# A hybrid attention and expert block on one core: x by feature columns instead of token rows, and half of its normalisation moved into the first block of experts

## The reference

```python
xn = rmsnorm(h, ln)              # h = meta tokens and x; y = x * rsqrt(mean(x*x) + 1e-6) * gain
proj = xn @ w_in                 # q, k, v of both attentions (stick-breaking, sliding window)
o = concat(rmsnorm(o_a), rmsnorm(o_b)); h = h + o @ w_out
# then, in blocks of 128 tokens (peer_ffn):
q = tb @ w_query;  top 16 of 128x128 expert pairs for each of 8 heads -> 128 experts a token
act = gelu(u[idx] . tb);  out = sum(softmax * act * v[idx])
h = rmsnorm(h + out, final_norm)
```

## Time and profile before

| | |
|---|---|
| times of three runs | 2914.4, 2919.9, 2925.72 us |
| the profiled execution | 2919.07 us, its span 2917.0 us |
| mean granted clock of TensorE | 0.878 |
| busy share of the span | PE 76%, DVE 75%, POOL 45%, ACT 39% |
| the chain that ended last, by engine | DMA 33%, PE 29%, DVE 23%, ACT 8%, issue 4%, POOL 2% |
| moved | 1155.22 MB, of which the gathers 1073.81 MB |

### The profile page before, as it was taken

How to read it: one execution, slowest core, us unless ns; L and a number is a source line. 1 busy time by engine, 2 the same in 40 slices (tenths; PEclk the granted TensorE clock), 3 DMA queues, 4 the chain that set the end, 5 groups by cost and what they waited for, 6 DMA issues and landing times.

```text
span 2917.0 us, 30220 instructions
## 1 busy us (share of the span) xinstructions
PE 2214.7 (76%) x9182; PEld 950.5 (33%) x9182; DVE 2184.8 (75%) x5506; ACT 1145.3 (39%) x2673; POOL 1316.1 (45%) x1126
## 2 busy tenths in 40 slices
PE   9989888788887988867887777867755775665556
PEld 7564532345333453313322332212311231111111
DVE  4189887786777868679786888779776987668555
ACT  3523377433563335633575326733212331121111
POOL 0024355444554435544565445644444444444442
PEclk9999999899999999979998898988877898767778
DMA  8279999999999999999999999999999999999997
GB/s 320 95 303 409 386 410 418 401 412 380 412 397 419 411 398 414 366 419 419 419 415 417 421 413 409 408 410 418 421 420 422 420 404 421 418 421 411 422 421 321
DMA packets 198096, 1155.22 MB, mean 396 GB/s; under 512 B 23648, under 2 KB 53792, under 8 KB 66480
## 3 DMA queue, kind: packets, MB, share of 16 engines
q0 software_dynamic: 147456, 1073.81, 89.6%
q1 hardware_dynamic: 50480, 79.50, 7.5%
HBM read 1138.21 MB, written 15.01 MB: 395 GB/s over the span
## 4 chain that ended last, share of the span: by engine, by line
DMA 33%; PE 29%; DVE 23%; ACT 8%; issue 4%; POOL 2%; SPq 0%; ACTq 0%; DVEq 0%; POOLq 0%
DMA r_uv<-in_experts,r_wk 31%; PE ps L1868 13%; DVE r_uv L1430 11%; PE ps L1540 4%; PE ps L1786 2%; ACT r_uv L1016 2%; PE ps L1764 2%; PE ps L1534 2%; ACT L1013 2%; POOL r_uv L756 1%; DVE r_wk L1201 1%; DVE r_wk L1199 1%; DVE r_wk L1202 1%; PE ps L1556 1%; DMA r_wk<-lq_dram 1%
## 5 line engine op out<-in xcount | busy, mean ns | idle before, releaser
L756 POOL DMA_INDIRECT r_uv<-in_experts,r_wk x1024 | 1212.8, 1184 | 1406.1 <-PE ps L1868 1191.8
L1868 PE MATMUL ps<-r_uv 128*64 128x512 f32 x4096 | 1234.5, 735 | 668.6 <-ACT r_uv L1016 655.8
L1430 DVE CUSTOM_DVE_ANT_0 r_uv<-r_uv,hnrep 128x1024 f32<-128x1024 f32 x1024 | 1253.8, 1240 | 548.4 <-DMA r_uv<-in_experts,r_wk 539.4
L1868 PEld LDWEIGHTS ps<-r_uv 128*64 128x64 f32 x4096 | 291.1, 157 | 1409.7 <-ACT r_uv L1016 943.9
L1013 ACT ACTIVATE r_wk<-r_wk 128x2 f32<-128x2 f32 x512 | 103.9, 203 | 1446.5 <-DVE r_wk L1430 1445.0
L1016 ACT ACTIVATE r_uv<-gid,r_wk 128x64 f32<-128x64 f32 x684 | 200.7, 340 | 11.6 <-ACT r_wk L1013 0.3
L1013 ACT ACT_TABLE_LOAD x138 | 177.1, 1283 | 2.5
L777 ACT ACT_TABLE_LOAD x117 | 150.1, 1283 | 8.1 <-PE ps L1744 3.7
L1540 PE MATMUL ps<-r_uv,stream_chunk 128*128 128x256 f32 x560 | 134.1, 394 | 3.8 <-DMA stream_chunk<-in_w_chunks 3.8
L1786 PEld LDWEIGHTS ps<-r_wk,r_wq 128*128 128x128 f32 x1024 | 119.6, 193 | 37.0 <-issue 36.5
L1786 PE MATMUL ps<-r_wk,r_wq 128*128 128x128 f32 x1024 | 128.7, 280 | 0.3 <-ACT r_wk L933 0.3
(11 more groups left out here) (181 smaller groups left out, 2217.1 us busy)
## 6 DMA issues: line engine op xcount, KB each, us to landing
r_uv<-in_experts,r_wk POOLq DMA_INDIRECT x1024, 13.5
stream_chunk<-in_w_chunks SPq DMA_DIRECT2D x30, 512.0 KB, 8.0
r_wk<-lkv_dram SPq DMA_DIRECT2D x72, 128.0 KB, 7.5
r_uv<-in_x SPq DMA_DIRECT2D x8, 512.0 KB, 10.3
r_wo<-in_w_chunks SPq DMA_DIRECT2D x8, 512.0 KB, 11.1
r_wk<-in_x SPq DMA_DIRECT2D x8, 512.0 KB, 8.2
r_wo<-in_w_out SPq DMA_DIRECT2D x8, 512.0 KB, 9.5
r_wq<-in_w_query SPq DMA_DIRECT2D x8, 512.0 KB, 6.8
```

What stands on the lines that cost most here:

```text
L756: g.indirect_dma_start(uv[:, SLOT[G], :], None, experts, bass.IndirectOffsetOnAxis(idx[b % 2][:, k:k + 1], 0)).then_inc(rows_in[SLOT[G]], 16)
L1430: v.tensor_tensor_reduce(uv[:, slot, 0:D], uv[:, slot, 0:D], hnrep[:, k % GRP, :], 1.0, 0.0, ALU.mult, ALU.add, actv[:, k:k + 1]).then_inc ...
L1868: last = t_.matmul(ps[HALF * j:HALF * j + HALF, i, :], uv[:, slot, 0:HALF], uv[:, slot, D + 512 * i:D + 512 * i + 512], start=n == 0, stop ...
```

## The change

x is given twice: as before, for the residual, and by columns, features on the partitions (`first_columns` for the tokens 0 to 255 and the meta tokens, `columns` for the other 768). A transposition on PE is not needed any more. ACT squares the columns; PE sums the squares over the partitions with a matrix of ones, which leaves each token's sum on all partitions; ACT and DVE take the root of 128x272 or 128x256 equal rows; DVE scales the columns in place by gain and root. For tokens 256 to 511 DVE first adds the eight features of a partition, and PE sums once. The tokens 512 to 1023 are not touched in the first stage. Their columns (2 MB) are loaded into slots 2 and 3 in block 0, ahead of the keys of unit 13 (units count from 0); they are squared at groups 54 to 56, summed at 55 to 57, their root is taken at 58 and they are scaled at 60 and 61. `NARROW` falls from 56 to 46. The store to `xs_dram` and its load are gone.

```diff
-ONE_MORE, NARROW, WIDE = 43, 56, STREAM_BLOCKS * NG
+FAR_LOAD, FAR_ROOT, FAR_SCALE = 13, 58, (60, 61)
+FAR_SQUARES = {54: (0, 1, 2), 55: (3, 4), 56: (5, 6, 7)}
+FAR_SUMS = {n + 1: cs for n, cs in FAR_SQUARES.items()}
+ONE_MORE, NARROW, WIDE = 43, 46, STREAM_BLOCKS * NG
...
# SP
-            load_x(0)
+            for h in range(DC // 2):
+                e.dma_start(xn0[:, 2 * h:2 * h + 2, :], first_columns[:, 2 * h:2 * h + 2, :]).then_inc(x_in[h], 16)
+            load_chunk(0)
             e.dma_start(cst[:, :], consts).then_inc(consts_in, 16)
...
-                    e.dma_start(xs_dram, r_uv[:, 4 * D:8 * D]).then_inc(xs_out, 16)
...
+                    if (b, u) == (0, FAR_LOAD):
+                        gate(e, "sp", rows_used, NB + max(G for G in range(K) if SLOT[G] in (2, 3)) + 1)
+                        e.dma_start(xnT[:, 1:3, :, :], columns[:, 1:3, :, :]).then_inc(xs_in, 16)
...
# ACT
+            def square_first(h):
+                act.wait_ge(x_in[h], 16)
+                a.activation(sq_columns[0][:, 2 * h:2 * h + 2, :], xn0[:, 2 * h:2 * h + 2, :], ACT.Square).then_inc(squared, 1)
+            def root_columns(tb):
...
+                a.activation(r, sums, ACT.Ln, scale=1.0 / n, bias=epscol).then_inc(logged, 1)
+                act.wait_ge(logged, tb + 1)
+                a.activation(r, r, ACT.Exp, scale=-0.5).then_inc(rooted, 1)
...
+                if s == 2:
+                    square_next()
+                if s == 4:
+                    root_columns(1)
...
# DVE
+            polish_columns(0, ps[:, 2, 0:GW + META], D)
+            dve.wait_ge(consts_in, 16)
+            scale_columns(xn0, r_columns[0])
+            dve.wait_ge(squared, DC // 2 + 2)
+            v.tensor_reduce(sq_next_sum, sq_columns[1].rearrange("p c n -> p n c"), AX.X, ALU.add).then_inc(next_reduced, 1)
+            polish_columns(1, ps[:, 3, 0:GW], D)
+            scale_columns(xnT[:, 0, :, :], r_columns[1])
...
+                    if b == 0 and n in FAR_SCALE:
+                        h = FAR_SCALE.index(n)
+                        if h == 0:
+                            polish_columns(2, ps[:, 7, :], -D)
+                        scale_columns(xnT[:, 1 + h, :, :], r_columns[2][:, GW * h:GW * h + GW])
...
# PE
+            def sum_far(c):
...
+                gate(pe, "pe", far_squared, c + 1)
+                t_.matmul(ps[:, 7, :], negones, sq_far[c], start=c == 0, stop=c == DC - 1).then_inc(far_summed, 1)
...
-            idle_products(11)
-            for k in range(2):
-                turn_rows(k)
-            idle_products(6)
+            pe.wait_ge(ones_set, 1)
+            idle_products(12)
+            sum_first()
+            idle_products(12)
```

More of the change, by code:

```diff
@@ L240, in settle, with block_program @@
             self.n = 0
-def block_program(nc, x, meta, w_chunks, w_v, consts, rope_cs, w_out, sinks, w_query, keys_t, experts, out):
+def block_program(nc, x, first_columns, columns, w_chunks, w_v, consts, rope_cs, w_out, sinks, w_query, keys_t, experts, out):
     with ExitStack() as ctx:
@@ L417, in block_program @@
         gain_spread = sem("gain_spread")
[L418 to L420 removed]
+        ones_set, xs_in = sem("ones_set"), sem("xs_in")
+        x_in = [sem(f"x_in{i}") for i in range(DC // 2 + 1)]
+        squared, col_summed, xT_ready = sem("squared"), sem("col_summed"), sem("xT_ready")
+        logged, rooted, next_reduced = sem("logged"), sem("rooted"), sem("next_reduced")
+        far_squared, far_summed = sem("far_squared"), sem("far_summed")
         v_summed, v_kept, zeroed = sem("v_summed"), sem("v_kept"), sem("zeroed")
@@ L813, in keep_values @@
                     a.activation(own_values, ps[0:rows, 6, 0:P], ACT.Copy).then_inc(v_kept, 1)
-            for k in range(5):
-                square_rows(k)
+            for h in range(DC // 2):
+                square_first(h)
+            root_columns(0)
             def keep_piece(i):
@@ new lines, in scale_columns @@
+            def scale_columns(columns, r):
+                for c in range(DC):
+                    last = v.scalar_tensor_tensor(out=columns[:, c, :], in0=columns[:, c, :], scalar=lnmix[:, c:c + 1], in1=r,
+                                                  op0=ALU.mult, op1=ALU.mult)
+                    if columns is xn0:
+                        last.then_inc(xT_ready, 1)
+                if columns is not xn0:
+                    last.then_inc(xT_ready, 1)
+            polish_columns(0, ps[:, 2, 0:GW + META], D)
@@ L1955 @@
     given = [
-        ("x", np.asarray(x)[0]), ("meta", np.asarray(meta_tokens)), ("w_chunks", w_chunks),
+        ("x", x), ("first_columns", rows(np.concatenate([x[0:GW], np.asarray(meta_tokens)]).T)),
+        ("columns", rows(x[GW:].T).reshape(P, DC, -1, GW).transpose(0, 2, 1, 3)), ("w_chunks", w_chunks),
         ("w_v", rows(np.concatenate([m[:, w * i:w * i + w] for i in range(PAIRS) for m, w in ((va, P), (vb, FAR))], axis=1))), ("consts", consts),
```

160 lines of the change are left out of this document (77 added, 83 removed).

## The result

The changed kernel takes 2933.8 us (median of 14 runs, 2926.2 to 2949.9) against 2919.8 for the kernel before in the same session (2913.7 to 2930.3). The ratio is 1.0047, 95% interval 1.0031 to 1.0063: 13.7 us slower (0.0047 x 2919.9). 2917 was predicted, with a range from 2906 to 2930: the kernel became slower where a small gain was forecast.

The account below looks back on a forecast made before the run. Once gathers run, memory sets the pace; before, PE's list does. From the profiled 2919.07, minus 4.6 (start) plus 2.0 (late block 0) gives 2916.5; that execution was 0.8 under the median, so 2917, range 2906 to 2930.

Parts of the forecast that it names:

- The first stage, -4.6: Start of the kernel to the turned keys: earlier first piece and no transpositions, less the second sum's wait, 4.6 us earlier.
- The rival that the start gives more: First stage saves 8.9 us and the starved stretch of block 0 regains 3.0, giving 2908; chance 0.20.
- The second sum, +2.1: Behind the third piece in the first stage: PE waits 1.6 us for DVE's reduction and needs 0.46 for its product.
- the reason given with the bound: DVE's second-sum reduction reads with a step of 256 words, at a rate not shown; twice as slow adds 2.3 us.
- The ring, +1.7: Late in block 0: seven slots instead of nine for ten groups, some 50 us, cost 1.7 us.
- Unit 13, up to 8: Block 0: unit 13's keys land behind the 2 MB load, so PE may stand for up to 8 us.
- the cover: Late in block 0: about 7.8 us of transfers queued ahead of a gather, hiding shorter stalls if the queue has refilled.
- The late part as a whole, +2.0: Late block 0: fewer slots, keys behind the load and bursts on ACT, PE and DVE together lose 2.0 us.
- far bound of 20: Late block 0 if nothing is hidden: 8 us at unit 13 and 4 + 4 + 4 of bursts, 20 us lost.
- the late bursts outrun the queue: Rival: at unit 13 and from group 54 on, delays exceed the queue's cover, giving 2925 to 2935; chance 0.22.
- Blocks 1 to 7: Nothing is changed there; any loss in these blocks would show the forecast wrong.

Follow-up runs that it names:

- e3: Kernel before with seven slots instead of nine from group 46, nothing else changed: ratio 1.0015.
- e4: Kernel before with seven slots from group 46 and its 2 MB load moved ahead of unit 13's keys: ratio 1.0018.
- e5: Changed kernel with load and squares of tokens 512 to 1023, but without their sums, root and scaling: ratio 1.0007.
- e6: Changed kernel without DVE's polishing and scaling of tokens 512 to 1023; squares, sums and root stay: ratio 1.0033.
- e13: Changed kernel with nine slots to the end of block 0, no 2 MB load, and the late work done on query-weight columns: ratio 0.9995.
- e1: Changed first stage with the late part of the kernel before (nine slots until group 56, load behind last keys); tokens 512 to 1023 unnormalised: ratio 0.9994.
- e10: e8 with the keys table loaded ahead of chunk 8 and DVE polishing at step 12 from ACT's copy of the sum: ratio 0.9986.
- e14: Changed kernel's first stage and seven slots from group 46, without 2 MB load and without late work: ratio 0.9995.
- e12: Changed kernel's first stage with nine slots to the end of block 0, without 2 MB load and without late work: ratio 0.9985.
- e7: Changed kernel, complete, with the 2 MB load issued on ACT's queue at group 46 instead of SP's queue: ratio 1.0046.
- e2: Changed kernel without squares, sums, root and scaling of tokens 512 to 1023; seven-slot ring and early load stay: ratio 1.0021.
- e16: Changed kernel with its late work spread: one square at each of groups 49 to 56, root at 58, scaling over 59 to 62: ratio 1.004.
- e8: Kernel before with all x normalised by columns in the first stage, then stored and reloaded as before; second sum one piece later: ratio 1.0002.
- e9: e1 with PE's second sum of squares one piece later, behind the fourth piece: ratio 0.9991.

## Why the prediction was wrong, by its steps

The measured time lies 16.8 us over the forecast (2933.8 against 2917). By the ratios 13.5 of them belong to the late part (15.5 where 2.0 were forecast) and 2.8 to the start (1.8 kept to the end where 4.6 were forecast); the second of these is inside its interval.

**The first stage, -4.6: right where the clock holds, too large on the mean.** The sum was made for the turned keys. In twelve traces with this first stage they start at 42.4 us on the mean, in the three with the old one (before, e3, e4) at 45.2: 2.8 earlier. In four of the twelve (after, e5, e6, e13) the clock stays at 1.00 behind the hole of the second sum and the keys start at 40.7, 4.4 earlier; in the other eight it is 0.89 to 0.93 on the mean from 15 to 30 us, and they start at 42.6 to 43.8. The first gather is issued at 161.0 us on the mean against 165.5, 4.5 earlier, but not all of that is the change's: from the turned keys to the first gather PE's list takes 118.2 to 118.3 us in every one of these traces whose granted clock from 100 to 120 us is 1.00, 121.4 at 0.83 (before and e4) and 122.9 at 0.74 (e6). Of the 7.5 us between the two traces that were compared first, 3.2 go with that clock. Whether the change has a part in it no run shows. To the end e1 keeps 1.8 us (-2.3 to 5.8); e10, whose keys come 6.0 us earlier than the trace before has them, keeps 4.1. The rival that the start gives more is not borne out: the first idle products took 4.38 to 5.49 us and hold the sum as forecast.

**The second sum, +2.1: too small, for the reason given with the bound.** The strided reduction took 3.62 us where 2.3 was scaled from a contiguous one, and PE's hole is 2.62 instead of 1.6. What the prediction had not foreseen is the clock behind the hole: in e1 the pieces there took 15.45 instead of 14.40 us. The Trainium skill (SBUF — State Buffer, "Door 1: The DMA port swizzle") has a penalty for accesses that go on to a new 16-byte line each time. The reduction agrees in direction, 1.3 us on 2048 elements; that the lines are the cause is not shown.

**The ring, +1.7: not contradicted.** e3 has 4.4 (0.3 to 8.5), e14 over e12 2.9.

**Unit 13, up to 8: the wait is there, 5.60 us.** That the keys wait behind the 2 MB in SP's queue was right: on another queue the wait is gone (e7). The Trainium skill (DMA: Bandwidth & Descriptors, "Queues, rings and completion order") says that a ring's transfers are taken in order, and these rows agree. But moving the load did not bring the time back, and memory lost only 1.7 us there, so that at this place the cover mostly held.

**The late part as a whole, +2.0: this step failed.** The prediction put the uncovered parts at 4 us each on ACT, PE and DVE and then let the queue hide them, since a gather landed 12.7 us after its issue and 7.8 us of transfers stood ahead of it. Measured are 15.5 us (1.0047 against 0.9994 of e1, with 6 on either side), three quarters of the far bound of 20 that the prediction had named and not taken: some 8 for ring and load (e2 over e1; the old first stage has 5.3 for the same two, e4 over before) and some 8 for the late work (after over e2), each again with 6 on either side. What the queue was to hide is seen by memory: a share of 0.77 to 0.90 instead of 0.95 to 1.01 from 500 to 540 us. The rival "the late bursts outrun the queue" was the right one, with its place and its time, at a chance of 0.22.

Three things speak on what was wrong in it. The 12.7 us were the median of 440 to 540, which mixes two rings. With nine slots the kernel before has medians of 13.7 (460 to 480 us) and 15.3 (2000 to 2300). With seven, as the changed kernel has them from group 46, it has 9.7 (740 to 860) and, from 500 to 520 us:

```profile
r_uv<-in_experts,r_wk POOLq DMA_INDIRECT x6, 9.4
```

By the prediction's own sum 9.4 leave 4.5 us of cover, not 7.8. (From 480 to 500 us, with the 2 MB under way, the median is 14.7.) The cover was counted once for each burst, as if the queue filled again in between; but from 500 to 540 us the share never came back to 1. A slot is refilled only after PE's products, and behind the bursts these come late. And from 2000 to 2300 us the DMA engines are at 1.01 before and after: there is no spare rate with which to catch up. From the first dot product of group 65 to the end the two traces take 2369.5 and 2368.3 us, so next to nothing of the 10.7 us lost in the late stretch came back (over all traces that rest takes 2365.8 to 2380.4). Nor was "free time" of 0.8 us a group a place for work: spread over the groups 49 to 62 it cost about the same (e16). How much each of the three weighs is not shown.

**Blocks 1 to 7: nothing lost**, as forecast (420 and 421 GB/s, and the stretch behind group 65 just named). In the kernel before the DMA engines are at 9 tenths or more from the fourth of the 40 slices on, not from the third, in which the first gather is issued and which has 7.

**The head start at group 0, not foreseen and not the change's.** The changed kernel's lead of 7.5 us at the first gather is 1.8 at the first diagonals, because ACT stands 6.70 us ahead of its copy of the last queries. So it does in all sixteen later traces (6.69 to 7.27 us), with the old first stage too. ACT's rows of e3, and then of the trace before:

```profile
175.71 0.60 ACT L946 ACTIVATE r_wk<-ps 128x512 f32<-128x512 f32 x1 [6.86 <-remote]
```
```profile
173.82 0.60 ACT L946 ACTIVATE r_wk<-ps 128x512 f32<-128x512 f32 x1 [2.38 <-PE ps L1786]
```

It is the trace before that lacks a stall of some 4.5 us. Read pair by pair, the two traces would have charged it to the change.

**Open** stay the cause of that stall, where e3's 4.4 us go, which of the late steps cost what, and how much of the late work nine slots would hide: by the times it costs 2.9 us there, by the trace as much as with seven. A trace's late stretch and the time of its kernel do not always agree (e5, e13), so the 15.5 us as a whole are safer than any part of them.

## What to carry to other kernels

Where transfers set the pace, work moved beside them is not free because its engine shows idle time: count what stands in order behind each moved instruction until a slot is released, and take the cover from the very stretch, with the number of slots that it will have, once, not once a burst. Put added work where the transfers are not the bound: here the first stage took the same normalisation for under 1 us of PE (e10), and block 0 lost some 8 us by it. And look at a second trace of the kernel before, before a difference between two traces is given to the change.

## What the runs showed of the hardware

- A DVE reduction of 2048 elements with a step of 1 KB: 3.62 us; a contiguous one of 1664: 1.886.
- PE's clock after a hole of 2.62 us behind 10.6 us of pieces without a gap: in eight of twelve traces granted 0.89 to 0.93 on the mean from 15 to 30 us, so part of it at the lower of its two levels (1.2 GHz); in the other four 1.00, all of it at 2.4 GHz, as in the three traces without the hole (e8, e9, e10). In e1 the hole ends at 26.62 us, and the clock is 0.50 from 27 to 29.
- The same 118.2 us of PE's list from the turned keys to the first gather take 121.4 where the clock from 100 to 120 us is 0.83.
- Time from issue to landing of a gather of 1 MB in the kernel before: medians of 13.7 us (460 to 480 us) and 15.3 (2000 to 2300) with nine slots, of 9.4 (500 to 520) and 9.7 (740 to 860) with seven.
- ACT, idle 6.69 to 7.27 us at the same instruction in all traces but that of the kernel before, with the first gathers in flight.
